# A float32 three-block network on one core: input-weight chunks ordered one place earlier among the modulation weights, and a small bias product moved to the opening

## The reference

```python
for i in range(DEPTH):
    shift, scale, gate = adaln(c, ada_w[i], ada_b[i])        # silu(c) @ ada_w[i] + ada_b[i], in three parts
    cshift, cscale, cgate = adaln(c_ctx, ada_w[i], ada_b[i])
    h = rms_norm(x, pre_g[i]) * (1.0 + scale) + shift
    hc = rms_norm(xc, pre_g[i]) * (1.0 + cscale) + cshift
    ...
def project(t):                                              # block 0: w_in is a_w_in, 1024 x 4096
    p = t @ w_in
    q, k, v, z = jnp.split(p, ...)
...
bias = rel_bias[t5_bucket(idx - qpos[None, :, None])]        # third block, rel_bias is 32 x 8
logits = logits + jnp.transpose(bias, (0, 3, 1, 2))
```

## Time and profile before

| | |
|---|---|
| median of 3 runs | 778.44 us (777.95 to 778.50) |
| the profiled execution | 778.1 us, span 776.1 us |
| PE busy in it | 763.7 us, 98% of the span |
| DVE, ACT, POOL busy | 553.0, 392.1, 42.0 us |
| moved by DMA | 125.71 MB, 162 GB/s in the mean |
| TensorE's granted clock | 1.00 |

### The profile page before, as it was taken

How to read it: one execution, slowest core, us unless ns; L and a number is a source line. 1 busy time by engine, 2 the same in 40 slices (tenths; PEclk the granted TensorE clock), 3 DMA queues, 4 the chain that set the end, 5 groups by cost and what they waited for, 6 DMA issues and landing times.

```text
span 776.1 us, 11232 instructions
## 1 busy us (share of the span) xinstructions
PE 763.7 (98%) x4137; PEld 614.3 (79%) x4137; DVE 553.0 (71%) x990; ACT 392.1 (51%) x749; POOL 42.0 (5%) x55
## 2 busy tenths in 40 slices
PE   8999999999999999999999999999999999999998
PEld 6777777877777888867888888787788888888886
DVE  3546998987677867599767776998977554554553
ACT  4542123238788765556566656634544444434341
POOL 1020000000001010111100002200100000000000
PEclk9999999999999999999999999999999999999999
DMA  9997355333000085149221144952325855665511
GB/s 319 359 397 257 132 217 195 116 119 115 1 1 1 1 333 206 57 164 351 93 72 56 49 149 171 366 206 104 113 68 173 271 163 166 209 207 180 208 61 55
DMA packets 72409, 125.71 MB, mean 162 GB/s; under 512 B 2858, under 2 KB 36860, under 8 KB 71204
## 3 DMA queue, kind: packets, MB, share of 16 engines
q1 hardware_dynamic: 71520, 123.00, 46.0%
q10 hardware_dynamic: 388, 1.08, 0.4%
q0 software_dynamic: 448, 0.92, 0.3%
HBM read 123.92 MB, written 1.06 MB: 161 GB/s over the span
## 4 chain that ended last, share of the span: by engine, by line
PE 69%; DVE 17%; SPq 5%; DMA 3%; ACT 3%; issue 2%; POOL 0%; DVEq 0%; ACTq 0%
PE psum L884 14%; PE psum L886 13%; PE psum L885 13%; DVE w_lo L2033 5%; PE psum L1093 3%; DMA raw<-in_a_w_in 3%; PE psum L1118 3%; SPq L653 3%; PE psum L1414 3%; PE psum L1413 3%; PE psum L1412 3%; PE psum L1010 3%; PE psum L1189 2%; PE psum L873 2%; PE psum L874 2%
## 5 line engine op out<-in xcount | busy, mean ns | idle before, releaser
L885 PE MATMUL psum<-w_lo,act_hi 128*128 128x512 f32 (+1 forms) x624 | 242.1, 388 | 0.0
L884 PE MATMUL psum<-w_hi,act_hi 128*128 128x512 f32 (+1 forms) x584 | 236.3, 405 | 1.2 <-DVE w_lo L2033 0.8
L886 PE MATMUL psum<-w_hi,act_lo 128*128 128x512 f32 (+1 forms) x584 | 226.8, 388 | 0.0
L2033 DVE TENSOR_TENSOR w_lo<-raw,w_hi 128x2048 fp32r<-128x2048 f32 (+1 forms) x68 | 153.2, 2260 | 65.0 <-ACT w_hi L1451 65.0
L1451 ACT ACTIVATE w_hi<-raw 128x2048 fp32r<-128x2048 f32 (+1 forms) x72 | 136.2, 1895 | 68.1 <-PE psum L886 30.2
L884 PEld LDWEIGHTS psum<-w_hi,act_hi 128*128 128x128 f32 x584 | 109.7, 188 | 33.7 <-issue 11.4
L885 PEld LDWEIGHTS psum<-w_lo,act_hi 128*128 128x128 f32 x624 | 117.5, 188 | 20.1
L886 PEld LDWEIGHTS psum<-w_hi,act_lo 128*128 128x128 f32 x584 | 109.6, 188 | 23.2
L2002 POOL TENSOR_TENSOR rstd<-ms,half_neg 128x1 f32<-128x1 f32 (+3 forms) x38 | 35.5, 937 | 519.1 <-DVE ms L2074 519.1
L873 PE MATMUL psum<-act_hi,w_hi 128*128 128x512 f32 x128 | 50.6, 396 | 3.2 <-DVE w_lo L2033 3.2
L874 PE MATMUL psum<-act_lo,w_hi 128*128 128x512 f32 x128 | 49.9, 390 | 0.0
(11 more groups left out here) (302 smaller groups left out, 1126.6 us busy)
## 6 DMA issues: line engine op xcount, KB each, us to landing
raw<-in_a_w_in SPq DMA_DIRECT2D x15, 1024.0 KB, 7.3
raw<-in_ada_w SPq DMA_DIRECT2D x12, 1024.0 KB, 5.2
raw<-in_w_out SPq DMA_DIRECT2D x12, 1024.0 KB, 5.7
raw<-in_w_gate SPq DMA_DIRECT2D x22, 512.0 KB, 4.1
raw<-in_w_up SPq DMA_DIRECT2D x22, 512.0 KB, 5.1
raw<-in_w_down SPq DMA_DIRECT2D x11, 1024.0 KB, 5.0
raw<-in_b_w_in SPq DMA_DIRECT2D x10, 1024.0 KB, 7.8
raw<-in_w_in SPq DMA_DIRECT2D x10, 1024.0 KB, 5.8
```

The lines of the kernel that those rows point to most:

```text
L884: pe.matmul(oh, x_hi, hi, start=(k == 0), stop=False)
L885: pe.matmul(o[:, 0:n], x_hi, lo, start=False, stop=False)
L886: mm = pe.matmul(oh, x_lo, hi, start=False, stop=(k == KT - 1))
L2033: ins = dve.tensor_tensor(rest, weights, hi.bitcast(F32), ALU.subtract)
```

## The change

In `loads_plan` the two halves of chunk c+1 stand ahead of the modulation piece that goes behind chunk c, for c = 1 to 3. Load numbers (two to each entry), with the slot n mod 6 in brackets:

| | 4,5 | 6,7 | 8,9 | 10,11 | 12,13 | 14,15 | 16,17 | 18,19 |
|---|---|---|---|---|---|---|---|---|
| slots | [4,5] | [0,1] | [2,3] | [4,5] | [0,1] | [2,3] | [4,5] | [0,1] |
| before | piece 1 | chunk 2 | piece 2 | chunk 3 | piece 3 | chunk 4 | gate | chunk 5 |
| now | chunk 2 | piece 1 | chunk 3 | piece 2 | chunk 4 | piece 3 | gate | chunk 5 |

`gate_place` and `ada1_place` are issued behind chunk 2. At the end of chunk 0, ACT and DVE split half 4 as well (`ahead=4`). The bias product, its copy and its write to DRAM stand in the opening; the operands lie in `gate0`, so DVE's first `gate_block` also waits for the write (`s_toepw`), and one filler of four products is gone.

```diff
@@ loads_plan @@
     for c in range(8):
-        plan += both("in0", c)
+        if c == 0 or c - 1 not in range(1, 4):
+            plan += both("in0", c)
+        if c in range(1, 4):
+            plan += both("in0", c + 1)
@@ banks_plan @@
+    put(("bias",), 5)
     for t in range(NT):
         put(("in0", 0, t), [0, 1, 7, 5][t])
...
-    put(("bias",), 6)
@@ memory @@
-        onehot = v_flat[0:32, 3072:3584]
-        toep = v_flat[0:HEADS, 3584:4096]
+        onehot = gate0[0:32, 1, 0:COLS]
+        toep = gate0[0:HEADS, 1, COLS:]
@@ sync @@
+            load(relb[:], a["rel_bias_2"], s_onehot)
+            load(onehot, a["k_onehot"], s_onehot)
             modulation(1)
...
             modulation(3)
+            b, at = place[("bias",)]
+            sp.wait_ge(free[b], at + 1)
+            sp.dma_start(toep_dram, toep).then_inc(s_toepw, 16)
             for n in range(2, len(loads)):
-                if loads[n] == ("in0", 2, 0):
+                if loads[n] == ("ada1", 1, 0):
 
                     b, at = place[("ada0", 1, 0)]
                     sp.wait_ge(full[b], at + 1)
                     for h in range(2):
                         load(gate_place[h], half_src("ada0g", 0, h)[0], s_gatein)
-                if loads[n] == ("ada1", 1, 0):
-
                     sp.wait_ge(s_xn, xn_base["norm0"] + NT)
...
-                if loads[n] == ("in2", 0, 0):
-                    ...
-                    load(onehot, a["k_onehot"], s_onehot)
-                if loads[n] == ("in2", 3, 0):
-                    ...
-                    sp.dma_start(toep_dram, toep).then_inc(s_toepw, 16)
@@ tensor @@
             ada_half("ada0", 1, 0)
-            stay_awake(5, 4)
+            pe.wait_ge(s_onehot, 32)
+            o = begin(("bias",))
+            pe.matmul(o[0:HEADS, :], relb[:], onehot, start=True, stop=True).then_inc(bank_full(("bias",)), 1)
             norm0_part(0, 1)
...
             gemm_unit("out1", 1, 1, SECOND)
-            pe.wait_ge(s_late, 16 * N_LATE)
-            pe.wait_ge(s_onehot, 16)
-            o = begin(("bias",))
-            pe.matmul(o[0:HEADS, :], relb[:], onehot, start=True, stop=True).then_inc(bank_full(("bias",)), 1)
@@ scalar @@
             norm0_square(3)
+            move(toep, ("bias",))
...
             for c in range(5):
-                run_chunk("in0", c, unit_in0, ahead=3)
+                run_chunk("in0", c, unit_in0, ahead=3 if c else 4)
...
-            move(toep, ("bias",))
@@ gpsimd @@
-                             (w_ukv[:, 0, :], a["w_uk_2"][0]), (w_ukv[:, 1, :], a["w_uv_2"][0]),
-                             (relb[:], a["rel_bias_2"])):
+                             (w_ukv[:, 0, :], a["w_uk_2"][0]), (w_ukv[:, 1, :], a["w_uv_2"][0])):
@@ vector @@
                         dve.wait_ge(s_gatein, 32)
+                        dve.wait_ge(s_toepw, 16)
...
             for c in range(5):
-                run_chunk("in0", c, unit_in0, ahead=3)
+                run_chunk("in0", c, unit_in0, ahead=3 if c else 4)
```

More of the change, by code:

```diff
@@ L454, in block_kernel @@
         s_ada1in = sem("second_layer_modulation_in")
-        N_CIN, N_VEC, N_LATE = 3, 4, 10
+        N_CIN, N_VEC, N_LATE = 3, 4, 9
         mrow1g = gate0[:, 0, :]
@@ L699, in _ @@
                     load(gain3, a["norm2_w_2"][0].partition_broadcast(P), s_gain3)
-                if loads[n] == ("in2", 0, 0):
-                    b, at = place[("pv1", XT * HEADS - 1)]
-                    sp.wait_ge(full[b], at + 1)
-                    load(onehot, a["k_onehot"], s_onehot)
-                if loads[n] == ("in2", 3, 0):
-                    b, at = place[("bias",)]
-                    sp.wait_ge(free[b], at + 1)
-                    sp.dma_start(toep_dram, toep).then_inc(s_toepw, 16)
                 if loads[n] == ("in2", 5, 0):
```

## The result

The changed kernel takes 806.93 us (median of 4 runs, 805.81 to 807.64), the kernel before 778.47 us beside it (4 runs, 777.95 to 778.62). The ratio is 1.0366, with a 95% interval of 1.0351 to 1.0382: slower by 3.7%, 28.5 us. The profiled execution took 807.2 us, with a span of 805.1 us against 776.1.

The account below looks back on a forecast made before the run. PE, busy 98% of the span, was taken as the bound. The profiled 778.1 - 3.3 (gains) + 0.2 (opening) + 8.5 (modulation waits) + 17.4 (chunk 5) + 2.7 (clock) = 803.6 us, range 798 to 810.

Parts of the forecast that it names:

- the ring: Load slots: a load waits for its slot's previous user, so pieces 2, 3 and chunk 5's first half come late.
- the four places: PE's new waits: modulation pieces behind chunks 2 and 3, chunk 5's start, and its fifth k block.
- rival (a): Slow clock at every wait, behind the modulation pieces too: plus 5.4, so 809.0 us; chance 0.15.
- What went in the chunks: PE's waits for DVE in chunks 2 and 3 go, minus 1.54 and minus 0.85 us; the one at 55.30 stays.
- The opening: Bias product replaces four fillers; a DMA comes later by 65 KB: plus 0.2 us, between minus 0.1 and plus 1.0.
- The modulation waits: Behind chunks 2 and 3, PE waits landing time L minus 0.80: 4.1 and 4.4 us, together plus 8.5.
- Chunk 5: Late half 10 costs 7.0 us at the start, DVE's work behind it a 9.6 us wait; plus 17.4 in all.
- The clock: Slow matmuls after idle: 2.7 us charged once, behind chunk 5's wait of 9.6 us; bounds 0 and 8.1.
- The bias gain: Third block: the moved bias product frees PE for 0.94 us, all taken as gain; at worst 0.
- (b): Rival: only the modulation waits cost, as DVE's chunk 4 work fits in behind: 783.5 us; chance 0.08.
- (c): Rival: ring not felt, pieces 2 and 3 in time, only the three gains remain: 775.0 us, faster; chance 0.04.
- (d): Rival: chunk 2 lands no earlier because the opening keeps DMA full, both small gains stay away: 806.0 us; chance 0.05.

Follow-up runs that it names:

- the ring with other slots: Changed kernel with pieces 2, 3 and gate in slots 0 and 1, odd chunks in 2 and 3, even in 4 and 5, another issue order: 776.58 us.
- The split-late kernel: Changed kernel with the split of half 10 on ACT and DVE moved from behind tile (4, 0) to ahead of tile (4, 3): 797.76 us.
- Fillers alone: Changed kernel with its new PE waits filled by products nobody reads, at pieces 2 and 3 and twice in chunk 5: 801.26 us.

## Why the prediction came out as it did

The forecast was 803.6 us with a range of 798 to 810; measured were 806.93 us. Sign, the ring, program order on DVE and the four places were right, and the time lies within the range. It does not lie within the forecast's own bounds of 800.3 to 806: the upper one left out the clock's upper bound of 8.1 us, and only rival (a) carried the range to 810. That the miss is no larger is in part luck, since terms of 5.8 us that were too small or absent met 2.4 us of small ones the other way. The terms, one by one:

**What went in the chunks: right, 0.6 us more than said.** The waits at 82.69 and 107.72 are gone and the one of 0.81 us stayed, now at 54.92. Chunk 2 runs 1.84 us shorter, where 1.54 was said. The row's idle time counts from the shown end of the matmul ahead, 0.39 us after its start, while in a row without pause the next starts after 0.23. So a wait of 1.54 in brackets costs 0.16 more, and some 0.1 for the slower start behind it (0.50 in its row instead of 0.39). By the same reading the 0.85 us at chunk 3 are worth 1.1; in the ring with other slots 1.15 go there.

**The opening: 0.6 us below what was said, in part scatter.** Plus 0.2 was said, with bounds of minus 0.1 and plus 1.0; minus 0.38 is the shift at chunk 2. Of it 0.20 stand already at 10 us, ahead of anything that the change touches (9.89 against 10.09): the first sixteen fillers took 5.38 us in this execution and 6.29 in the one before, and PE then waited 0.6 us longer for a DMA. The rest, minus 0.2, is a little below the lower bound.

**The modulation waits: right.** L minus 0.80 gave 4.1 and 4.4. The shift grows by 5.21 us over piece 2 (from -2.22 to +2.99) and by 5.06 over piece 3; 0.9 of each is the slow second half, which leaves 4.3 and 4.1. The halves landed 4.9 to 5.0 us after their issue. The order of the ring, read from SP's rows before, was enough to place the waits and to size them.

**Chunk 5: right.** 7.0 us at its start were said and 7.1 measured: the shift of 17.36 less the 10.26 that chunk 4 ends late (161.30 against 151.04). At the fifth k block 9.6 were said. The row shows 7.86 of idle, but the twelve matmuls ahead of it took 1.6 us longer at the low clock, and the wait hid that; the shift grows by 26.98 - 17.36 = 9.62. Behind it, the prediction let DVE's delay count, which was 0.8 us more than PE's there (17.4 against 7.0 + 9.6). That did not come: DVE reached attention 27.7 us late (its reciprocal of 174.54 in the earlier trace rows stands at 202.27), PE 29.3, because of the clock; the two delays lay side by side instead of adding up. DVE's work between its two rests is 12.44 us, against 12.3. The split-late kernel confirms this step.

**The clock: the step that failed.** It charged 2.7 us once and nothing behind the modulation pieces, because their idle stretches of some 2 us "are nearer to the 1.54 row". Behind each piece the second half costs 0.9 us more (1.86 from its start to the next matmul's, for 0.93), and the first matmuls of the next chunk 1.6 to 1.7: the shift grows over chunk 4 from 8.55 to 10.26, and over chunk 3 from 2.99 to 3.49 although a wait of 0.85 (1.1, as above) had gone. That is 5.2 us for the two pieces, near the 5.4 of rival (a). Behind chunk 5's second wait it is 26.98 to 29.25, 2.3 us, where 2.7 were charged; the low level near 180 us that was to confirm the term is there, 0.50 from 176 to 184. The 2.7 was a stand-in, read from the kernel's first sixteen products, beside which the profile shows a granted clock of 1.00 (2 to 6 us). It was also a little large: the 6.29 us run to the end of the sixteenth product, so the like at full pace is 15 x 0.227 + 0.39 = 3.8 and not 3.63, which gives 2.5. The clock measures 7.5 us in the ledger instead of 2.7. Fillers alone gave back 5.7 of it in the medians; they leave short waits, and in its profiled execution the opening was a microsecond later. The Trainium skill, page "TensorE: Matmul & The Clock Gate", section "HAM oscillation — how this bites in real kernels", says of a matmul kernel with a DMA wait in each step of its loop that TensorE was throttled anew in every one. The trace agrees at the two pieces, which wait for DMAs and have 0.50 behind them both times; at chunk 5 the same follows waits for DVE. The prediction cited it and gave the rival that goes with it a chance of 0.15; the row of 1.54 us, a single case, had been given too much weight.

**The bias gain: failed too.** Minus 0.94 was taken whole and 0 came (the shift is +28.93 just ahead of the product's old place, 494.86 against 465.93, and +28.91 behind), the end that the prediction named as "at worst". Its cause is DVE, as shown. The rows that would have told it were in the trace of before: DVE's end 0.06 us ahead of PE's start.

Together: clock plus 4.8, bias plus 0.9 and chunk 5's start plus 0.1 stand against the opening (minus 0.6), the gains of chunks 2 and 3 (minus 0.6), the modulation waits (minus 0.1), DVE's delay that did not add up (minus 0.8) and 0.3 given back between the first of attention and the third block (29.25 to 28.93), the cause of which was not followed. That leaves 3.4, and 3.5 is the difference between the growth of the span, 29.0, and the 25.5 foreseen.

**The rivals.** (a) had the mechanism of the clock and nearly its size; its 809.0 is 2 us too high for the smaller terms above. It speaks of four places and charges three; the fourth, ahead of the longer wait of chunk 5, is indeed hidden (1.6 us). (b) is refuted by the two waits of chunk 5, (c) by the six waits. But the 775.0 us of (c) are close to what the ring with other slots measured, 776.6. (d) is refuted by ACT, which rounds half 4 at 52.84, where it did at 66.33 in the earlier trace rows.

## What to carry to other kernels

Where buffers are handed out by place in a list, moving an entry earlier changes which transfer waits for which consumer; write down for each load who must be done before it can be issued, and who stands right behind that in time. Two users that follow each other directly on the bound engine should not share a slot: here that put two waits of some 4 us on it. The price of a late load is not its wait alone: add the work that stands in program order behind the instruction that waits for it (here it cost 9 us), and the slow clock wherever the idle time lowers it (here 2.3 us behind one long wait, 2.6 behind a pair of short ones). And a gain on one engine is taken only after a look at how early the next partner was: here 0.06 us.

## What the runs showed of the hardware

The granted clock fell behind idle stretches that the prediction had held for harmless. A single stretch of 1.74 us in one kernel, and one of 2.28 us in another, was followed by some 3 us at 0.50. After 1.54 us in the kernel before and after 1.61 and 1.92 us in the openings of two other kernels it stayed at 1.00. So the length of a single stretch does not decide it alone, and what else does is not settled here, as no run set idle stretches of several lengths in one place: the same waits at piece 2 and piece 3 let the clock fall ahead of the half behind them in one case and after it in the other. At the low level a matmul of 512 columns starts 0.43 us after the one before, instead of 0.23. And idle time in brackets understates a short wait on PE by 0.2 to 0.3 us.
